# Rows of the last token chunk requested two context blocks later, in one core's fused mixer layer

## The reference, cut to what matters

```
h = rmsnorm(x, rms_g) * (1 + scale) + shift        # per token, then per channel
q, k, v, z_a, glu, z_b, gates = split(h @ w_in + b_in)   # w_in: 1024 x 5632
```

## Time and profile before

| | us |
|---|---|
| median of 3 runs | 1723.22 (1723.14 to 1723.63) |
| the profiled execution, its own time | 1724.99 |
| its span in the trace | 1723.4 |
| TensorE busy | 1701.1 (99%) |
| VectorE busy | 1242.2 (72%) |
| ScalarE busy | 862.1 (50%) |
| GpSimdE busy | 653.6 (38%) |
| moved by DMA | 286.31 MB, mean 166 GB/s |

### The profile page before, as it was taken

The page is one execution under the profiler, slowest core; times in us unless marked ns, Lnnn a source line. Parts: engine busy times, 40 slices in busy tenths (PEclk is TensorE's granted clock), DMA queues, the critical chain, the costliest instruction groups (busy, mean ns, idle before and its releaser), DMA issues.

```text
span 1723.4 us, 27674 instructions
## 1 busy us (share of the span) xinstructions
PE 1701.1 (99%) x9909; PEld 1442.6 (84%) x9909; DVE 1242.2 (72%) x1789; ACT 862.1 (50%) x1501; POOL 653.6 (38%) x509
## 2 busy tenths in 40 slices
PE   8999999999999999999999999999999999999998
PEld 5787888888899988888888888889898888888886
DVE  3785888788757858888687856777777665677776
ACT  3553434455567644434544437777779222333443
POOL 0044675565200026856555653224223100005443
PEclk9999999999999999999999999999999999999999
DMA  9443534333598734444333368988666777673442
GB/s 325 126 150 126 135 124 143 93 92 110 178 309 262 211 96 129 155 132 111 98 127 100 104 172 219 230 205 209 167 146 172 247 231 234 191 261 134 148 158 86
DMA packets 271644, 286.31 MB, mean 166 GB/s; under 512 B 49960, under 2 KB 217748, under 8 KB 268309
## 3 DMA queue, kind: packets, MB, share of 16 engines
q1 hardware_dynamic: 271106, 284.18, 56.0%
q10 hardware_dynamic: 403, 0.37, 0.1%
HBM read 203.18 MB, written 81.30 MB: 165 GB/s over the span
## 4 chain that ended last, share of the span: by engine, by line
PE 86%; DMA 4%; DVE 3%; issue 2%; POOL 2%; ACT 1%; SPq 1%; POOLq 0%; ACTq 0%; DVEq 0%
PE banks L1837 38%; PE banks L2391 6%; PE banks L2965 4%; PE banks L2967 4%; PE banks L2966 4%; DMA w_raw<-in_w_in 3%; PE banks L3025 3%; PE banks L3027 3%; PE banks L3026 3%; PE banks L2355 2%; PE banks L1967 2%; PE banks L1966 2%; PE banks L1965 2%; PE banks L2361 2%; PE banks L2331 1%
## 5 line engine op out<-in xcount | busy, mean ns | idle before, releaser
L1837 PE MATMUL banks<-a_hi,w_hi 128*128 128x512 f32 x1176 | 460.2, 391 | 0.8 <-ACT out_stage L1117 0.4
L1837 PE MATMUL banks<-a_hi,w_lo 128*128 128x512 f32 x1176 | 457.8, 389 | 0.0
L1837 PE MATMUL banks<-a_lo,w_hi 128*128 128x512 f32 x1176 | 457.7, 389 | 0.0
L1506 DVE SCALAR_TENSOR_TENSOR banks<-glu_out,taps,banks 128x1009 f32<-128x1009 f32 (+1 forms) x240 | 342.2, 1426 | 5.2
L1837 PEld LDWEIGHTS banks<-a_hi,w_hi 128*128 128x128 f32 x1176 | 220.8, 188 | 50.0 <-issue 3.6
L1837 PEld LDWEIGHTS banks<-a_hi,w_lo 128*128 128x128 f32 x1176 | 220.8, 188 | 46.4
L1837 PEld LDWEIGHTS banks<-a_lo,w_hi 128*128 128x128 f32 x1176 | 220.9, 188 | 45.0
L1006 POOL TENSOR_TENSOR t_raw<-w_raw 128x512 f32<-128x512 f32 x39 | 53.6, 1373 | 400.6 <-DMA w_raw<-in_w_in 394.4
L1425 DVE SCALAR_TENSOR_TENSOR w_lo<-w_raw,w_hi 128x1024 fp32r<-128x1024 f32 x84 | 108.9, 1296 | 104.9 <-ACT w_hi L1097 103.6
L960 POOL TENSOR_TENSOR w_lo<-t_raw,w_hi 128x1024 fp32r<-128x1024 f32 x70 | 171.6, 2461 | 23.7 <-ACT w_hi L1097 21.4
L2503 ACT ACTIVATE probs<-scores,stat 128x640 f32<-128x640 f32 (+2 forms) x128 | 106.6, 833 | 51.2 <-DVE stat L2425 49.8
(11 more groups left out here) (282 smaller groups left out, 3678.6 us busy)
## 6 DMA issues: line engine op xcount, KB each, us to landing
w_raw<-in_w_in SPq DMA_DIRECT2D x34, 1024.0 KB, 5.7
cw_raw<-in_w_in SPq DMA_DIRECT2D x44, 512.0 KB, 5.0
proj<-out_stage SPq DMA_DIRECT2D x80, 256.0 KB, 2.3
gates_in<-proj SPq DMA_DIRECT2D x64, 256.0 KB, 3.0
k_hi<-k_hi_rows SPq DMA_DIRECT2D x16, 640.0 KB, 11.5
k_lo<-k_lo_rows SPq DMA_DIRECT2D x16, 640.0 KB, 13.5
q_split<-q_rows SPq DMA_DIRECT2D x8, 1152.0 KB, 6.0
w_ada<-in_w_ada SPq DMA_DIRECT2D x8, 1024.0 KB, 11.2
```

The lines of the kernel that those rows point to most:

```text
L1506: op = dve.scalar_tensor_tensor(dst, src, by, dst, ALU.mult, ALU.add)
L1837: op = pe.matmul(out, x[w][:, b, k], y, start=(start and k == j == 0), stop=(k == H - 1 and j == 2), skip_group_check=not start)
```

## The change

Both requests for the rows of chunk 3 are issued two blocks later: the first half at block 7 and not at block 5, the second at block 9 and not at block 7. Nothing else is changed.

```diff
@@ -868,8 +868,8 @@ front_sync
             if BLOCK_UNIT[n] == i:
                 for m in LOAD_AFTER[n]:
                     load_block(sp, m)
-                if n in (5, 7):
-                    load_x(sp, 3, n - 5)
+                if n in (7, 9):
+                    load_x(sp, 3, n - 7)
                 if n == LAST_USE[0]:
                     load_pair(sp, NQ1)
             store_unit(sp, i)
```

## The result

Timed against each other in 22 executions each, the changed kernel takes a median of 1726.94 us (1722.92 to 1731.59) and the kernel before 1723.32 us (1722.24 to 1727.55). The ratio is 1.0019 with a 95% interval of 1.0013 to 1.0024, so the change costs 3.3 us (2.2 to 4.1). The profiled execution took 1727.89 us for a span of 1726.3 us, 2.9 us more than before's 1724.99 and 1723.4.

The account below looks back on a forecast made before the run. TensorE, busy 1701.1 of 1723.4 us, was taken as the bound; its idle 0.68 + 0.95 us becoming about 0.8 + 2.5 adds 1.6 us, giving 1724.8 us on the median of 1723.22, range 1722.4 to 1727.0.

Parts of the forecast that it names:

- its cover: Before block 12's transpose: slab ready at 515.0, wanted at 515.51, so ScalarE's first wait costs TensorE nothing.
- the sum: TensorE's idle time before chunk 3: 0.68 + 0.95 us become about 0.8 + 2.5, +1.6 us, not given back.
- the likeliest time, 1724.8 us: Case A, chance 0.54: two short ScalarE waits passed on by a full VectorE, +0.09% on the median.
- the range: 1722.4 to 1727.0 us, from C's lower part to A's upper bound, leaving out B and D's far side.
- rival D: SP only 0.6 us ahead, second half landing at 523.6, ScalarE 4.5 us late: 1727.1 us; chance 0.14.
- Case C: It evens out: SP 3.3 us ahead, second half landing at 519.5, within 0.5 us of 1723.2; chance 0.20.
- VectorE's full queue as the carrier: ScalarE's late cached-key copy makes VectorE 1.7 us later; its full queue passes this to the last normalization and turn(32).
- The rule on one transfer: Skill's fit, about 2.0 us plus bytes at 436 GB/s: 1 MB lands after 4.4 us, before ScalarE asks.
- Rival B: Transfers hidden, landing after 5.1 us; ScalarE never waits, both idle moments go: -1.63, 1721.6 us; chance 0.12.

Follow-up runs that it names:

- delay kernels: Kernel before, requests unmoved, with two or four chained zero writes on VectorE ahead of chunk 3's last normalization; ratios 1.0008 and 1.0019.
- pool_after: Changed kernel with the four normalizations of chunk 3 on GpSimdE in place of VectorE; ratio 1.0009, +1.6 us on the kernel before.
- poolhalf_after: Changed kernel with the first two tiles of chunk 3 normalized on GpSimdE, the last two on VectorE; ratio 1.0024, +4.1 us on the kernel before.
- the fills: 24 or 12 identity transposes in TensorE's idle time on the changed kernel (1.0027, 1.0018), and 24 on the kernel with four VectorE writes (1.0024).
- delay1: Kernel before with two chained zero writes on VectorE ahead of chunk 3's last normalization; ratio 1.0008, +1.4 us.
- delay2: Kernel before with four chained zero writes on VectorE ahead of chunk 3's last normalization; ratio 1.0019, +3.3 us.
- pool_before: Kernel before with the four normalizations of chunk 3 on GpSimdE in place of VectorE; ratio 1.0003.
- one_later: Changed kernel with both requests one block later still, at blocks 8 and 10; ratio 1.0036, +6.2 us on the kernel before.
- second_only: Kernel before with only the second half moved, to block 9, the first staying at block 5; ratio 1.0021, +3.6 us.

## Why the prediction was half right

**Right, with the mechanism.** SP is 2.8 us ahead at block 7 (forecast 2.8); the requests go at 504.5 and 511.4 us (504.8 and 512.4); they land at 513.5 and 521.35 (513.1 and 521.4), since two errors cancel: each landing took 0.7 to 1.0 us longer than I had taken it, and the requests went 0.3 and 1.0 us earlier. ScalarE waits 3.0 and 1.3 us (2.4 and 1.7 to 2.3), VectorE's waits for stores are gone, and turn(32) comes at 533.58 (533.3). TensorE has no idle time over 0.2 us before block 12's transpose; its cover was put at half a microsecond and was 0.15 us, and moving the requests one block more used it up. The idle time grows by 1.59 us where the sum has 1.6 (its own terms, 0.8 + 2.5 for 0.68 + 0.95, make 1.7; measured were 0.53 + 2.69). The loss needs the second request late, as the text says: with the first alone at its new place nothing was lost.

**Wrong: a term is missing from the sum.** The step that failed is "0.68 + 0.95 us of TensorE's idle time become about 0.8 + 2.5, that is +1.6 us, and nothing behind gives it back". It prices idle time at its own length. One idle time of 2.69 us in place of two under 1 us also halved TensorE's clock behind it, which costs 1.5 us more in the profile and 1.4 in the mean of the timed executions. With that term the sum is 1.6 + 1.5 = 3.1 us against 3.3 measured. So the likeliest time, 1724.8 us, was 2.1 us too low against the median of 1726.94. That this median lies in the range, just inside its upper end of 1727.0, is luck: the end was drawn for a later landing, not for a slower clock. The page and the windows before couldn't show the term, because no idle time of the rows was long enough; the 1.00 of the granted clock in the earlier trace rows beside idle moments of 0.68 and 0.95 us says only that those were free. In numbers the result looks like rival D (1727.1), but D's mechanism did not happen: SP was 2.8 us ahead, not 0.6, and the landing was at 521.35, not 523.2 or later. Case C was no better: the drained queue did give back 2.8 us of the delay, but the landings went to their long end.

**Half right: VectorE's full queue as the carrier.** I argued that the last normalization is late because ScalarE's copy holds a VectorE that is full from there on. The delay kernels show the last link, that a late normalization on VectorE reaches turn(32), and relieving VectorE altogether may have taken some of the cost away (pool_after). But in the changed kernel itself the low part of the cached keys starts 1.4 us later than before (524.21 against 522.82) and the last normalization 1.9 us later; the sum had 1.7 for both. Between them VectorE stands again, 0.45 us at 525.08, for ScalarE's rounding. And poolhalf_after, with VectorE less loaded, lost as much as the changed kernel: ScalarE is late for more than one of VectorE's operations.

**The rule on one transfer.** By the fit of the Trainium skill (DMA: Bandwidth & Descriptors, Anatomy of one DMA) 1 MB lands after an estimated 4.4 us; the changed kernel's two requests took 9.0 and 10.0 us in a stretch with a DMA share about 1.0. Rival B, which needed a landing near 5 us, is out.

**Open.** Why the fills regain the clock and not the time. Whether the medians of delay1 and delay2 (+1.4 and +3.3 us, for writes of 1.1 and 2.5 us on VectorE) contain a whole step of the clock can't be told: their columns of clock loss stand 0.8 and 1.1 us above before's, each with an error of 0.3 to 0.4, where a fall in every execution would make 1.7. That executions of the kernel before pay the step already fits badly, since its 2.3 us leave little for falls once the end of the program is taken off; only one of its executions was profiled.

## What to carry to other kernels

On an engine that is 99% busy, don't add up idle time as if every microsecond were worth the same: ask whether several short gaps merge into one long one, since here each gap of 2.03 us and more took another 1.3 to 1.5 us with it through TensorE's clock, and gaps up to 1.54 us took nothing more than themselves. Before a request is moved back, set its landing under load, at the long end of what the rows show, against the moment of first use: here 9 to 10 us of landing left the second request no cover, and the first 0.15 us. And before a remedy is believed from one good profile, time it: three kernels here had a stretch over 2 us shorter than their partner's and were not faster.

## What the runs showed of the hardware

- In the profiles of these fourteen kernels, from 20 us on, no idle time of TensorE of 0.24 to 1.54 us was followed by a lower clock (the 1.54 us stands in pool_before at 765.04 and in one_later at 771.44). Each of 2.03, 2.37, 2.45, 2.45, 2.50, 2.67, 2.69 and 3.38 us has a granted clock of 0.50, 1.2 GHz, behind it, and cost 1.3 to 1.5 us whatever its length. Nothing between 1.54 and 2.03 us occurred. In the first 20 us, where TensorE often stands, the clock fell in five of the fourteen.
- Busy time hides it: TensorE was 1.00 busy in each of those windows. The count of matmuls gives it away, 11 or 12 in 2 us against 19 at full clock. The mean granted clock over many executions shows it too (0.99864 against 0.99782), but it also holds the low clock at the end of the program, where TensorE has nothing left to do.
- GpSimdE multiplies 128x1024 fp32 by a column in 2.9 to 3.5 us (5.84 to 7.05 us for two tiles; VectorE 0.75 for one), and some of VectorE's own operations beside it took twice as long (a low part of a slab 1.41 to 1.48 us instead of 0.69).
- A request can hold the queue of its issuing engine for very different times: a 1 MB request for x took 0.61 us to 3.22 us to issue, a store of proj 0.47 us (the changed kernel at 514.62) to 3.83 us (second_only at 502.26). That earlier transfers still in flight make the difference is what the rows suggest; no run here isolates it.
